# Second feed-forward part of a two-block network: inner tiles finished on VectorE and ScalarE instead of GpSimd

## The reference

```
def dwconv3(x, w, b):
    xp = jnp.pad(x, ((0, 0), (1, 1), (0, 0)))
    return xp[:, :-2] * w[0] + xp[:, 1:-1] * w[1] + xp[:, 2:] * w[2] + b

def conv_ffn(h, w_in, conv_w, conv_b, w_out):
    a = dwconv3(h @ w_in, conv_w, conv_b)
    gate, up = jnp.split(a, 2, axis=-1)
    return (jax.nn.silu(gate) * up) @ w_out
```

## Time and profile before

| | |
|---|---|
| median of 3 runs | 2080.07 us (2079.8 to 2082.15) |
| the profiled execution, its own time | 2080.6 us, of which the span is 2078.9 us |
| mean granted TensorE clock | 0.977 of full |
| busy: TensorE matmul | 1969.3 us (95%) |
| busy: VectorE | 1249.3 us (60%) |
| busy: ScalarE | 939.3 us (45%) |
| busy: GpSimd | 288.3 us (14%) |
| layer 1's feed-forward part | about 1062 to 1267 us of the span |
| chain that ended last: TensorE / VectorE / ScalarE / GpSimd | 83% / 7% / 4% / 1% |

### The profile page before, as it was taken

How to read it: one execution, slowest core, us unless ns; L and a number is a source line. 1 busy time by engine, 2 the same in 40 slices (tenths; PEclk the granted TensorE clock), 3 DMA queues, 4 the chain that set the end, 5 groups by cost and what they waited for, 6 DMA issues and landing times.

```text
span 2078.9 us, 33997 instructions
## 1 busy us (share of the span) xinstructions
PE 1969.3 (95%) x13365; PEld 1745.7 (84%) x13365; DVE 1249.3 (60%) x1809; ACT 939.3 (45%) x1464; POOL 288.3 (14%) x245
## 2 busy tenths in 40 slices
PE   5999989999999899999979998999999999989998
PEld 3776747778888489989969997998899999879997
DVE  6355355543654545667567676656975566787564
ACT  4344445322332332258466455346654444565353
POOL 2000113430542000021024140000010010000001
PEclk9999989999999899999989999999999999989999
DMA  8621464433223523222434544542344544324553
GB/s 356 214 78 61 162 223 154 171 115 118 83 87 104 182 101 123 82 81 82 145 126 157 186 162 138 183 149 82 134 159 173 181 166 143 110 87 168 183 182 122
DMA packets 43950, 296.77 MB, mean 143 GB/s; under 512 B 4976, under 2 KB 6128, under 8 KB 11696
## 3 DMA queue, kind: packets, MB, share of 16 engines
q1 hardware_dynamic: 36576, 247.48, 34.5%
q10 hardware_dynamic: 6048, 42.49, 5.9%
q0 software_dynamic: 1200, 5.02, 0.6%
HBM read 293.93 MB, written 1.05 MB: 142 GB/s over the span
## 4 chain that ended last, share of the span: by engine, by line
PE 83%; DVE 7%; ACT 4%; DMA 2%; issue 2%; POOL 1%; SPq 0%; ACTq 0%; DVEq 0%; POOLq 0%
PE acc L456 23%; PE acc L458 22%; PE acc L457 22%; DVE w_lo L393 2%; PE acc L451 2%; PE wk L570 2%; PE acc L452 2%; PE acc L453 2%; PE wk L1599 1%; DMA ada_first<-in_w_ada 1%; PE wk L730 1%; ACT w_hi L383 1%; PE wk L593 1%; DMA ada_ring<-in_w_ada 1%; PE wk L1329 1%
## 5 line engine op out<-in xcount | busy, mean ns | idle before, releaser
L456 PE MATMUL acc<-Hhi,w_hi 128*128 128x272 f32 (+2 forms) x2304 | 745.5, 324 | 31.1 <-DVE Hlo L772 9.1
L458 PE MATMUL acc<-Hhi,w_lo 128*128 128x272 f32 (+2 forms) x2304 | 721.9, 313 | 0.0
L457 PE MATMUL acc<-Hlo,w_hi 128*128 128x272 f32 (+2 forms) x2304 | 721.2, 313 | 0.0
L393 DVE TENSOR_TENSOR w_lo<-w_raw,w_hi 128x1024 fp32r<-128x1024 f32 (+2 forms) x472 | 586.8, 1282 | 201.1 <-ACT w_hi L383 199.5
L383 ACT ACTIVATE w_hi<-w_raw 128x1024 fp32r<-128x1024 f32 (+2 forms) x472 | 452.6, 1005 | 436.0 <-PE acc L458 356.7
L456 PEld LDWEIGHTS acc<-Hhi,w_hi 128*128 128x128 f32 x2304 | 441.9, 192 | 77.1 <-issue 36.6
L457 PEld LDWEIGHTS acc<-Hlo,w_hi 128*128 128x128 f32 x2304 | 442.3, 192 | 21.7
L458 PEld LDWEIGHTS acc<-Hhi,w_lo 128*128 128x128 f32 x2304 | 441.7, 192 | 22.5
L456 PE MATMUL acc<-Fhi,w_hi 128*128 128x256 f32 (+2 forms) x864 | 264.7, 306 | 5.1 <-POOL Flo L1086 5.1
L458 PE MATMUL acc<-Fhi,w_lo 128*128 128x256 f32 (+2 forms) x864 | 264.4, 306 | 0.0
L457 PE MATMUL acc<-Flo,w_hi 128*128 128x256 f32 (+2 forms) x864 | 264.1, 306 | 0.0
(11 more groups left out here) (381 smaller groups left out, 2432.8 us busy)
## 6 DMA issues: line engine op xcount, KB each, us to landing
w_raw<-in_w_ffn_in SPq DMA_DIRECT2D x44, 1024.0 KB, 4.9
ada_ring<-in_w_ada ACTq DMA_DIRECT2D x40, 1024.0 KB, 4.9
w_raw<-in_w_mlp_in SPq DMA_DIRECT2D x32, 1024.0 KB, 4.8
w_raw<-in_w_mlp_out SPq DMA_DIRECT2D x32, 1024.0 KB, 4.9
w_raw<-in_w_ffn_out SPq DMA_DIRECT2D x32, 704.0 KB, 4.0
ada_first<-in_w_ada SPq DMA_DIRECT2D x8, 1024.0 KB, 18.1
w_raw<-in_w_ret_v SPq DMA_DIRECT2D x8, 1024.0 KB, 4.7
w_raw<-in_w_ret_g SPq DMA_DIRECT2D x8, 1024.0 KB, 4.8
```

What stands on the lines that cost most here:

```text
L393: dve.tensor_tensor(w_lo[:, r, a:b], w_raw[:, r, a:b], w_hi[:, r, a:b].bitcast(F32), ALU.subtract).then_inc(lo_done, 1)
L456: pe.matmul(o, w_hi[:, r, w], x_hi(k), start=k == 0, stop=False)
L457: pe.matmul(o, w_hi[:, r, w], x_lo(k), start=False, stop=False)
L458: mm = pe.matmul(o, w_lo[:, r, w], x_hi(k), start=False, stop=k == last)
```

## The change

In layer 1 alone, both halves, `act_ffn_in` and `dve_ffn_in` are replaced by `act_ffn_in_alone` and `dve_ffn_in_alone`, and `pool_ffn_in` is not called. VectorE makes the product of slot s - 1 after `split_lo` of slot s, and the difference `F_lo` of slot s - 1 at the end of slot s. ScalarE copies `hid` to `F_hi` between the middle terms and the Silu of the next slot. The product is computed once. The new functions are written with a Python loop over 11 slots, without the hardware loop. Layer 0's part stays as it was.

```
+            def high(s):
+                r = (p.slot0 + s) % 2
+                act.wait_ge(hid_mul, 2 * FFH + f0 + s + 1)
+                act.activation(F_hi[n][:, s, :], hid[:, r, 0:n], ACT.Copy).then_inc(conv_mid, 1)
+            for s in range(p.n):
+                st = Step(p, None, s)
+                split_hi(act, st)
...
+                if s >= 1:
+                    high(s - 1)
+                act.wait_ge(conv_gate, f + 1)
+                act.activation(sg[:, r, 0:n], cgu[:, r, 0, 0:n], ACT.Silu).then_inc(silu_done, 1)
+            high(p.n - 1)
...
+            def product(s):
+                r = (p.slot0 + s) % 2
+                dve.wait_ge(silu_done, f0 + s + 1)
+                dve.wait_ge(freed["dve"], p.freed0 + s + 1)
+                dve.tensor_tensor(hid[:, r, 0:n], sg[:, r, 0:n], cgu[:, r, 1, 0:n], ALU.mult).then_inc(hid_mul, 1)
+            def low(s):
+                r = (p.slot0 + s) % 2
+                dve.wait_ge(conv_mid, mid_count(half, s + 1, 2) if s + 1 < p.n else 4 * FFH + 3 * FFH * (half + 1))
+                dve.tensor_tensor(F_lo[n][:, s, :], hid[:, r, 0:n], F_hi[n][:, s, :].bitcast(F32), ALU.subtract).then_inc(hid_done, 1)
+            for s in range(p.n):
+                st = Step(p, None, s)
+                split_lo(dve, st)
+                f, r = s + f0, st.parity()
+                if s >= 1:
+                    product(s - 1)
...
+                if s >= 1:
+                    low(s - 1)
+            product(p.n - 1)
+            low(p.n - 1)
...
         def pool_ffn(pool, layer, r):
-            pool_ffn_in(pool, layer, 0)
-            pool_ffn_in(pool, layer, 1)
+            if layer == 0:
+                pool_ffn_in(pool, layer, 0)
+                pool_ffn_in(pool, layer, 1)
             pool_y_sum(pool, r)
```

More of the change, by code:

```diff
@@ L1087, in pool_hidden, with mid_count, act_ffn_in_alone @@
             each_slot(pool, p, slot)
+        def mid_count(half, st, c):
+            return 4 * FFH + 3 * FFH * half + (3 * st + c if st else 1 + c)
+        def act_ffn_in_alone(act, half):
+            p = proj[ffn_name(1, half, "in")]
+            n, f0 = p.T, (2 + half) * FFH
+            def high(s):
[6 more added lines that the diff above has]
+                f, r = s + f0, st.parity()
+                for c in range(2):
+                    act.wait_ge(acc_ready, st.tile(c))
+                    if c == 0:
+                        act.wait_ge(hid_done, f - 1)
+                    m = s + (22 * c + FFH * half)
+                    act.activation(cgu[:, r, c, 0:n], acc_tile(p, r, c), ACT.Identity,
+                                   bias=V("conv_b", m + 44), scale=V("conv_w", m + 4 * 44)).then_inc(conv_mid, 1)
+                if s >= 1:
[3 more added lines that the diff above has]
+            high(p.n - 1)
@@ new lines, in dve_ffn_in_alone @@
+        def dve_ffn_in_alone(dve, half):
+            p = proj[ffn_name(1, half, "in")]
+            n, f0 = p.T, (2 + half) * FFH
+            def product(s):
[10 more added lines that the diff above has]
+                split_lo(dve, st)
+                f, r = s + f0, st.parity()
+                if s >= 1:
+                    product(s - 1)
+                for c in range(2):
+                    dve.wait_ge(conv_mid, mid_count(half, s, c))
+                    o = cgu[:, r, c, 0:n]
+                    w = V("conv_w", s + (22 * c + FFH * half + 3 * 44))
+                    dve.scalar_tensor_tensor(o[:, 1:SEQ], acc_tile(p, r, c)[:, 0:SEQ - 1], w, o[:, 1:SEQ],
+                                             ALU.mult, ALU.add).then_inc(conv_left, 1)
+                for c in range(2):
+                    dve.wait_ge(conv_left, 2 * f + c + 1)
+                    o = cgu[:, r, c, 0:n]
+                    w = V("conv_w", s + (22 * c + FFH * half + 5 * 44))
+                    dve.scalar_tensor_tensor(o[:, 0:SEQ - 1], acc_tile(p, r, c)[:, 1:SEQ], w, o[:, 0:SEQ - 1],
+                                             ALU.mult, ALU.add).then_inc(conv_gate if c == 0 else freed["dve"], 1)
+                if s >= 1:
+                    low(s - 1)
+            product(p.n - 1)
+            low(p.n - 1)
@@ L2707, in act_ffn @@
             a = ADA_FIRST + ADA_FFN
-            act_ffn_in(act, layer, 0, after=(lambda s: act_ada(act, a + s, a + s + 1) if ADA_FFN + s < ADA_LATE else None)
-                       if layer == 0 else None)
+            if layer == 1:
+                act_ffn_in_alone(act, 0)
+            else:
+                act_ffn_in(act, layer, 0, after=(lambda s: act_ada(act, a + s, a + s + 1) if ADA_FFN + s < ADA_LATE else None))
             act_plain(act, ffn_name(layer, 0, "out"))
-            act_ffn_in(act, layer, 1)
+            if layer == 1:
+                act_ffn_in_alone(act, 1)
+            else:
+                act_ffn_in(act, layer, 1)
             act_y_squares(act, ffn_name(layer, 1, "out"), r)
@@ L2719, in dve_ffn @@
         def dve_ffn(dve, layer, r, link=None):
-            dve_ffn_in(dve, layer, 0)
+            if layer == 1:
+                dve_ffn_in_alone(dve, 0)
+            else:
+                dve_ffn_in(dve, layer, 0)
             dve_y(dve, ffn_name(layer, 0, "out"))
-            dve_ffn_in(dve, layer, 1)
+            if layer == 1:
+                dve_ffn_in_alone(dve, 1)
+            else:
+                dve_ffn_in(dve, layer, 1)
             if layer == 0:
```

## The result

| | before | after |
|---|---|---|
| median (lowest to highest) | 2079.8 us (2079.34 to 2082.15, 5 runs) | 2069.41 us (2068.42 to 2070.61, 5 runs) |
| ratio to before | | 0.9947, 95% interval 0.9935 to 0.9959 |
| profiled execution: own time, span | 2080.6, 2078.9 us | 2069.41, 2067.7 us |

What follows compares the result with a forecast made beforehand. TensorE's matmuls, filling 95% of the span, were taken as the bound. Terms 1.3 + 3.9 + 2.1 + 1.5 = 8.8 us off 2080.6 gave 2071.8, stated as 2072.0, range 2069.5 to 2077.5 us.

Steps and rivals of the forecast that it cites:

- Table loads: Ten loads in `ffn1_in0`'s loop become one; only those between Silu and `w_hi`, or ahead of the first `w_hi`, delay TensorE.
- The start: First stop of `ffn1_in0`: without the load ahead of the first `w_hi`, TensorE gains 1.3 us.
- Ring: ScalarE-VectorE turn per `in` slot shrinks from 5.93 to 5.49 us, under TensorE's 5.76; both halves gain 3.9 us.
- the row that I chose: Price of VectorE's product in each `in` slot: 0.42 us, from a 128x256 TENSOR_TENSOR with two SBUF inputs at 0.425 us.
- The rival that the short losses are TensorE's own: 0.18 us per slot of `ffn1_in1` is the price of TensorE's wait instructions and stays; 2073.6 us, chance 0.06.
- Ends: Ends of both halves, where TensorE waits for GpSimd's last `F_lo`: 1.06 us gained per end, 2.1 us for two.
- what is late next: Weight split of `out` slot 1, behind the last high copy, limits the gain per end to 1.06 us, not 1.9.
- Clock: Half-clock stretch after `ffn1_in0`'s 1.90 us stop disappears once the stop is about 0.6 us: 1.5 us, bounds 0 and 1.5.
- Rest: Earlier SyncE loads and straight code replacing ScalarE and VectorE loops: taken as 0, bounds 0 to 1 us for fetching.

Runs made afterwards that it cites:

- run 8: The changed kernel, unedited, profiled for one more execution: 2069.44 us.
- Run 4: Changed kernel with a one-column Silu on ScalarE ahead of the first `w_hi` of `ffn1_in0`, putting one table load back there: 2071.95 us, ratio 0.9957.
- run 1: Kernel before, with layer 1's ScalarE and VectorE in-projection loops written straight, GpSimd's work left as it was: 2076.94 us, ratio 0.9982.
- run 2: Changed kernel with GpSimd doing three instructions per slot on scratch memory, which nothing waits for: 2082.55 us, ratio 1.0004.
- run 12: Kernel before, delayed by repeating 36 matmuls in the last slot of `ffn1_out1`, same result: 2082.13 us.

## Why the prediction was right and wrong

**Table loads: right.** One load is left in `ffn1_in0`. The start gave 1.4 us for 1.3: counted from the first matmul of `ffn1_in0`, `w_hi` starts at 5.89 us instead of 7.30. These 1.41 us are the load's 1.28 and 0.13 more, since without the load `w_hi` starts 0.1 us before the copy ahead of it has ended. The stop itself says less (0.84 us here, 0.43 in run 8), because slot 0 ends earlier or later with its own slow clock; slot and stop together are 8.33 to 8.37 us in every execution without the load. Run 4 took the start and the clock back with one load.

**Ring: right.** 5.93 us became one under TensorE's 5.76; both halves lost their stops, 2.83 + 1.03 us. Runs 1 and 2 show the two halves of it apart: the loads are worth 4.2 us of the part (with the clock), and GpSimd's quiet is what makes room for the product. The product took 0.42, the row that I chose. The rival that the short losses are TensorE's own is refuted by every slot of the changed kernel from slot 2 on: 5.76 us.

**Ends: right, with "what is late next".** 1.1 us per end for 1.06. The working by the late split was needed: GpSimd's wait alone would have promised 1.9.

**Clock: right in size, 1.5 us, but the reason given for it does not hold throughout.** The prediction has the fall follow from the stop of 1.90 us. In all ten executions here without the load ahead of `w_hi` (stops of 0.43 to 0.88 us) slot 1 takes 5.82 or 5.83 us, at full clock. Of the four with it, three took 7.2 to 7.3 us, and in the fourth, run 12, the clock did not fall behind a stop of 1.57 us. There it fell behind GpSimd's stop of 1.99 us at the end of the half, where the prediction had seen no fall, and that cost 1.5 us:

```profile
1138.00:1140.00 2.00, 2.00 (x12) 2.00 (x11) 1.17 (x2) 1.47 (x2) 0.00 (x0) 0.50 0.90 307
```

In run 2 it fell behind a stop of 0.88 us in `ffn1_out1`. So the length of the stop alone does not tell whether the clock falls, and that the term came whole in this pair is in part luck.

**Rest: the step that failed.** Under *Rest* I took 0, with bounds of 0 to 1 us for fetching alone, and the sum took all outside the part as unchanged; in the range I let runs vary by 1 us. The rest was 2.3 us shorter in one pair of profiles and 3.1 in another. Of these 2.2 and 2.3 us stand behind the part, and one stage 600 us later, where TensorE waits in short pieces and the clock falls or not, gives 2.6 and 3.0 (other places take a little back). 2078.9 - 8.9 - 2.3 = 2067.7 us, the span. The forecast of 2071.8, given as 2072.0 for a clock term that might not come each time, was thus 2.4 us too high (2.6 as given), and the lower bound of 2069.5 left next to nothing for a gain beyond the part. I can't foretell such shifts from the diff: 4.3 us of delay took 1.7 us off what stands behind the part in the kernel before, 8.8 us put 2.3 on that of the changed one. They belonged into the range, on both sides: in the profiles here that change nothing outside the part the rest goes from 1863.7 to 1867.8, so some 2 us each way.

## What to carry to other kernels

Before moving work to a quiet engine, look whether its work slows a neighbour beneath it: here 44 small instructions more on VectorE cost TensorE nothing in the `in` slots, since VectorE's large ones, with two SBUF inputs, became 0.85 us cheaper per slot. The two table loads inside this hardware loop were paid again each time round; ask of each load what stands ahead of it. And give a forecast for a long kernel a term for stages that are only moved: delaying the same work by 0, 4, 9 and 13 us changed what came behind it by up to 2.6 us.

## What the runs showed of the hardware

- A weight split pair of 128x1024 with two SBUF inputs takes 2.36 us alone and 3.2 to 3.4 while GpSimd's instructions run beside it (before, runs 1 and 2), whose own 128x256 ones take 1.10 us in the mean of run 2 and 0.74 where VectorE does little.
- An ACT_TABLE_LOAD takes 1.28 us in every row, and the next instruction starts 0.01 to 0.02 us behind it where nothing else is awaited. Ahead of `w_hi` it put `w_hi` off by 1.41 us.
- A stop of TensorE costs 0.07 to 0.1 us more than its own length, in the distance of the second matmul behind it (0.19 to 0.23 instead of 0.12).
- The same 18 matmuls of 256 columns in a row take 3.83 us at half clock and 2.14 at full; half clock over short waits cost far less: 6.8 us of it in the c stretch of run 8 made no more time than 3.4 in the changed kernel.
- The clock stayed full behind a stop of 1.57 us (run 12) and fell behind one of 0.88 us (run 2), so in these runs the length of a stop alone does not tell.
